# Attention heads and the closing stage of a two-layer trunk: one product moved ahead, value products in two banks, more banks and buffers at the end

## The chip, the cores and the metric

The kernel runs as one program on one core of a Trainium2 chip. The metric is the device time of one execution in microseconds (us), taken as the median of several runs. Five engines work side by side and are ordered by semaphores alone: TensorE (PE; its weight loads are shown apart as PEld), VectorE (DVE), ScalarE (ACT), GpSimd (POOL) and SyncE (SP), which here only issues DMA transfers.

## The reference

One step of a diffusion trunk with two layers over 128 prompt tokens and 512 sample tokens of width 1024, all in fp32. Layer 0 mixes by retention, layer 1 by attention; each is followed by a mixture of 16 experts, of which a router takes two for each token. Only the attention and the end of the step matter here.

```python
q = (rmsnorm(cq, q_norm) @ w_uq).reshape(B, T, MLA_HEADS, MLA_NOPE + MLA_ROPE)
...
k_nope = jnp.einsum('bkr,rhd->bkhd', ckv, w_uk)
v = jnp.einsum('bkr,rhd->bkhd', ckv, w_uv)
...
s = jnp.einsum('bqhd,bkhd->bhqk', qn, k_nope) + jnp.einsum('bqhd,bkd->bhqk', qp, kpe)
p = jax.nn.softmax(s.astype(F32) * scale, axis=-1).astype(v.dtype)
return jnp.einsum('bhqk,bkhd->bqhd', p, v)
...
return o @ w_o
...
xs = xs + g2s * grouped_moe(...)
y_sample = rmsnorm(xs, norm_final)
```

There are 8 heads of 128 columns (and 64 rotary ones), 640 tokens in five tiles of 128, the fifth being the prompt, which reads only its own 128 keys.

## The kernel before

The program is written engine by engine; each engine executes its list in order, and every `wait_ge` on a semaphore stands in that list. PSUM has eight banks of 512 fp32 columns, used under fixed numbers. The order of the work is written out by hand; there is no planner.

**A head of attention.** TensorE's list has for each head h three parts. `head_proj(h)` projects the queries of the 512 sample tokens into bank 1 (four steps of 128 rows, each two instructions of 512 columns, L1482); then the rotary queries into bank 2 (even heads alone, for two heads at once), the prompt's queries and the last 256 keys into bank 7, and the first 512 keys into bank 3. ScalarE (L1868, L1870) copies banks 1 and 3, VectorE banks 2 and 7 (for even heads with the rotation, L2476, then L2482 and L2487). `tail(h - 1)` closes the head before: the transposes of its fifth tile of probabilities and the value products of tiles 3 and 4. `main(h)` has the scores of the five tiles (L1513, L1514; even tiles in banks 0 and 1, odd ones in 2 and 3, the fifth only 128 columns in bank 0), the transposes of the first four tiles of probabilities (L1522, banks 4 and 5) and the value products of tiles 0 to 2 (L1532), in an order that puts other matmuls between a tile's scores and its transposes:

```python
score(h, 4)
prob_T(h, 3)
prob_v(h, 2)
```

is its end. Of a tile's softmax VectorE takes the maximum (L2493), ScalarE the exponential with its sum (L1878), TensorE transposes the result, ScalarE copies it out of PSUM (L1887), TensorE multiplies it by the values, and VectorE scales that by the reciprocal of the sum into `o_all` (`o_evac`, L2505). All value products are in bank 6, so each waits for the `o_evac` of the one before (`o_ev`). The SP list loads the next weights for keys and queries (`key_w`, `pair_w`) each time a head's projections are done.

**From the heads to the output projection.** After the tail of head 7, TensorE transposes `o_all` tile by tile into banks 2 and 3 (`o_T`, L1569); ScalarE and VectorE copy a half each (`oT_evac`, L1912 and L2539), and for each tile 32 instructions (L1581) project it into banks 4 and 5. VectorE's list has, between the last `o_evac` and its first `oT_evac`, `router_weights(1)` (L2011 to L2014). The SP list loads the gates' rows and the first expert's weights after the last value product (L672, L658 to L660).

**The last stage.** After the experts of layer 1, the SP list reads the sums back from DRAM into `x` (L707). The last expert's rows are spread by one-hot products, two banks for each tile in the pairs 4, 6, 2, 4, 6 (L1385); from the fourth tile on they wait for VectorE's add (`x_add`, L2393) to free a pair. ScalarE squares each tile (L1625), POOL makes the reciprocal root (`rstd`, L812 and L813), and VectorE's `final(t)` (L2409) scales the tile into one of two buffers, `fin`, which SP stores (L754). VectorE's list has all five adds first, then the five calls of `final`, each from the third on waiting until the store of its buffer's former tile has landed.

## Time and profile before

| what | value |
|---|---|
| runs of the kernel | 1773.40, 1774.48, 1776.93 us (median 1774.48) |
| span of the profiled execution | 1772.2 us |
| TensorE busy | 1684.3 us, 95% |
| VectorE, ScalarE, GpSimd busy | 705.7, 260.4, 184.0 us |
| attention heads | 1226 to 1444 us |
| output projection | 1449 to 1525 us |
| experts of layer 1 | 1555 to 1743 us |
| last stage | 1744 to 1772 us |

The profiled execution has its span alone on the page; how long that execution took as a whole is not shown. Times in the rows are counted from the start of the span. "Busy" is the time in which an engine had an instruction at work; matmuls overlap in a pipeline, so the time from one start to the next tells more than a matmul's own duration. An fp32 matmul shows as two instructions.

### The profile page before, as it was taken

To read this page: it belongs to the slowest core of one execution; us is meant where nothing else is said; L and a number is where in the kernel's file an instruction comes from. 1 tells how busy PE (TensorE), PEld (TensorE's weight loads), DVE (VectorE), ACT (ScalarE), POOL (GpSimd) and SP (SyncE) were. 2 spreads that over 40 slices of the span, in tenths; PEclk is the share of its full clock that TensorE was granted. 3 is DMA by queue.
4 is the path that set the end of the run, shared out by engine and by line. 5 is a ranking of instruction groups with operands and counts; after the bars stand their busy time and mean duration, and the time that the engine had idled before them with its cause. 6 is when DMAs were issued, how large, how long until landed. Compare 5 with 4: busy or idle time off the path is not lost.

```text
span 1772.2 us, 17375 instructions
## 1 busy us (share of the span) xinstructions
PE 1684.3 (95%) x6368; PEld 952.0 (54%) x6368; DVE 705.7 (40%) x1195; ACT 260.4 (15%) x554; POOL 184.0 (10%) x280
## 2 busy tenths in 40 slices
PE   5999999999999999999899999899999989999995
PEld 3864375644765465744464444354666654654442
DVE  1425533365333553255663232332233324533324
ACT  5100000000000000000121111322322321111111
POOL 2000100011000110001002222110000000022211
PEclk9999999999999999999999999999999999999998
DMA  8532561016410271103839999820000042579994
GB/s 320 204 142 95 199 224 48 0 48 235 156 47 0 95 286 57 47 0 141 256 149 307 351 339 329 273 100 3 22 25 11 0 120 95 201 244 343 340 329 143
DMA packets 159074, 280.21 MB, mean 158 GB/s; under 512 B 11396, under 2 KB 106392, under 8 KB 153896
## 3 DMA queue, kind: packets, MB, share of 16 engines
q1 hardware_dynamic: 144616, 236.39, 38.0%
q0 software_dynamic: 8960, 32.56, 7.0%
q10 hardware_dynamic: 5440, 10.49, 1.7%
q8 instruction: 36, 0.59, 0.1%
q14 instruction: 22, 0.18, 0.0%
HBM read 246.04 MB, written 33.37 MB: 158 GB/s over the span
## 4 chain that ended last, share of the span: by engine, by line
PE 79%; SPq 10%; DMA 4%; DVE 3%; issue 2%; ACT 2%; POOL 0%; DVEq 0%; POOLq 0%; ACTq 0%
PE banks L1085 11%; PE banks L1161 11%; PE banks L1060 8%; PE banks L1351 6%; SPq L659 5%; SPq L660 4%; PE banks L1482 4%; PE banks L1581 4%; PE banks L1157 3%; PE banks L1229 3%; PE banks L1368 2%; PE banks L1239 2%; PE banks L1217 2%; DMA wr<-in_moe_w_down 2%; PE banks L1513 2%; PE banks L1514 2%
## 5 line engine op out<-in xcount | busy, mean ns | idle before, releaser
L1351 PE MATMUL banks<-wr,arena 128*128 128x512 f32 x512 | 226.4, 595 | 10.8 <-DMA wr<-in_moe_w_down 10.1
L1161 PE MATMUL banks<-wr 128*128 128x512 f32 x432 | 191.4, 592 | 0.0
L1085 PE MATMUL banks<-wr 128*128 128x256 f32 x768 | 169.5, 379 | 0.0
L1351 PEld LDWEIGHTS banks<-wr,arena 128*128 128x128 f32 x512 | 94.6, 190 | 121.2 <-issue 118.9
L1085 PEld LDWEIGHTS banks<-wr 128*128 128x128 f32 x768 | 145.3, 190 | 22.7 <-issue 3.6
L1060 PE MATMUL banks<-wr,arena 128*128 128x512 f32 x320 | 143.4, 603 | 2.0 <-ACT arena L1688 2.0
L1161 PEld LDWEIGHTS banks<-wr 128*128 128x128 f32 x432 | 80.0, 190 | 91.2 <-issue 91.2
L1368 PE MATMUL banks<-wr,arena 128*128 128x512 f32 x256 | 115.4, 593 | 0.9 <-ACT arena L1804 0.9
L1060 PEld LDWEIGHTS banks<-wr,arena 128*128 128x128 f32 x320 | 60.5, 194 | 73.3 <-issue 72.3
L879 POOL DMA_INDIRECT acc_dram<-arena,put_ids x30 | 60.5, 2016 | 268.6 <-DVE arena L2363 268.6
L2348 DVE SCALAR_TENSOR_TENSOR arena<-banks,slot_w,arena 128x256 f32<-128x256 f32 x32 | 15.5, 484 | 173.6 <-ACT arena L1800 173.6
L2363 DVE TENSOR_TENSOR arena<-banks,arena 128x1024 f32<-128x1024 f32 x32 | 39.2, 1225 | 83.4 <-PE banks L1368 83.4
L1368 PEld LDWEIGHTS banks<-wr,arena 128*128 128x128 f32 x256 | 46.3, 190 | 48.3 <-issue 46.9
L1581 PE MATMUL banks<-wr,arena 128*128 128x512 f32 x160 | 70.2, 597 | 0.0
L829 POOL TENSOR_TENSOR arena<-arena 128x256 f32<-128x256 f32 x32 | 23.3, 733 | 377.6 <-DVE arena L2105 377.6
L2184 DVE BATCH_NORM_STATS2 st<-banks 128x6 f32<-128x512 f32 x40 | 28.0, 699 | 81.6 <-PE banks L1229 64.5
L2055 DVE TENSOR_TENSOR arena<-banks,arena 128x512 f32<-128x512 f32 x40 | 27.6, 691 | 82.3 <-PE banks L1060 82.2
L1229 PE MATMUL banks<-arena 128*128 128x512 f32 x128 | 60.1, 592 | 0.0
L1157 PE MATMUL banks<-wr 128*128 128x512 f32 x128 | 55.7, 593 | 0.0
L1482 PE MATMUL banks<-arena 128*128 128x512 f32 (+1 forms) x192 | 53.3, 434 | 1.1 <-DVE wr L2458 1.1
L1713 ACT ACTIVATE arena<-arena 128x512 f32<-128x512 f32 x24 | 15.1, 629 | 247.0 <-DVE arena L2164 114.1
L1581 PEld LDWEIGHTS banks<-wr,arena 128*128 128x128 f32 x160 | 30.4, 193 | 36.4 <-issue 36.4
(324 smaller groups left out, 2193.7 us busy)
## 6 DMA issues: line engine op xcount, KB each, us to landing
wr<-in_w_ada SPq DMA_DIRECT2D x24, 2048.0 KB, 7.6
wr<-in_moe_w_gate SPq DMA_DIRECT2D x32, 1024.0 KB, 14.2
wr<-in_moe_w_up SPq DMA_DIRECT2D x32, 1024.0 KB, 16.3
wr<-in_moe_w_down SPq DMA_DIRECT2D x32, 1024.0 KB, 15.6
wr<-in_ret_w_in SPq DMA_DIRECT2D x12, 2048.0 KB, 14.0
wr<-in_ret_w_in SPq DMA_DIRECT2D x8, 1024.0 KB, 11.7
wr<-in_ret_w_out SPq DMA_DIRECT2D x4, 2048.0 KB, 7.7
arena<-mod_rows_dram SPq DMA_DIRECT2D x14, 512.0 KB, 6.4
```

What stands on the lines that cost most here:

```text
L659: sp.dma_start(gu[:, :, 1, :], w_u[l][e]).then_inc(S(f"w_full{b}"), 16)
L660: sp.dma_start(dn, w_d[l][e]).then_inc(S(f"w_full{b}"), 16)
L879: g.indirect_dma_start(out=acc[l], out_offset=bass.IndirectOffsetOnAxis(ap=put_ids[:, e:e + 1], axis=0), in_=ysb[:, b, :], in_offset=None, ...
L1060: mm = mmul(bank[6 + hf][:], yT[:, t % 2, j, :], ring(slot)[:, j * D + hf * 512:j * D + hf * 512 + 512], start=(j == 0), stop=(j == 3))
L1085: mm = mmul(dst[:, r * 256:r * 256 + 256], lhs, rhs, start=(start and r == 0 and k == 0), stop=(k == 3), skip_group_check=True)
L1157: mm = mmul(dst, hT[:, k, TS:T], ring8(2 + int(tile))[:, k, :], start=(k == 0), stop=(k == KT - 1))
L1161: mm = mmul(dst, X[X_OF[p]][:, k, cols], W[p][:, k, :], start=(k == 0 and p not in ("P2", "P7", "P3")), stop=(k == 3), skip_group_check=True)
L1229: mm = mmul(bank[5][:], qd[:, u % 2, j, :], St[:, r, j, :], start=False, stop=(j == 1))
L1351: mm = mmul(bank[2][:], xgT[:, e.par, k, :], expert_w(e.buf)[0][:, k].rearrange("p g f -> p (g f)"), start=(k == 0), stop=(k == KT - 1))
L1368: mm = mmul(bank[4 + 2 * e.par + hf][:], gactT[:, e.par, j, :], expert_w(e.buf)[1][:, j, hf * 512:hf * 512 + 512], start=(j == 0), stop=(j ...
L1482: mm = mmul(dst, lhs(k), rhs(k), start=(k == 0), stop=(k == nk - 1))
L1581: mm = mmul(bank[4 + hf][:], oTb[:, t % 2, k, :], w_o[:, k, hf * 512:hf * 512 + 512], start=(k == 0), stop=(k == KT - 1))
```

## The change

It has four parts.

- `head_proj` is split: its stage 0, the query projection into bank 1 with the waits for the weights, moves into `main` of the head before, between the fifth score and the fourth transposes; stage 1 has the rest and, new, waits for the `o_evac` of tile 1.
- Value products use banks 6, 7, 6, 6, 7 (`PV_BANK`); each waits for the `o_evac` of the product that had its bank before, and that of tile 4 also for VectorE's evacuation of the next head's projections (`hp_d`), which share bank 7.
- After the last head, `o_T(0)` and the first `oT_evac` of ScalarE and VectorE come ahead of the tail, and `router_weights(1)` comes after VectorE's second `oT_evac`.
- In the last stage of layer 1 the bank pairs are 4, 6, 2, 0, 4, `fin` has five buffers, in tiles that are no longer used, and VectorE's list has `final(t - 2)` behind the add of tile t.

```diff
 V_BANK = (6, 7, 0, 1)
+PV_BANK = (6, 7, 6, 6, 7)
+LAST_BANK = ((4, 6, 2, 4, 6), (4, 6, 2, 0, 4))
...
+        def heads_d(h):
...
+            return 2 * h + 2
...
         def ring(s):
...
         fin_row = M["last"]
-        fin = M["xgT"].rearrange("p (b d) -> p b d", b=2)
+        fin = [xgT[:, 0].rearrange("p k n -> p (k n)"), xgT[:, 1].rearrange("p k n -> p (k n)"), xg[:, 0, :], xg[:, 1, :],
+               M["rows"][:, 0:D]]
...
                 dst = out[0][0] if t == PT else out[1][0, ORDER[t] * P:(ORDER[t] + 1) * P, :]
-                sp.dma_start(dst, fin[:, t % 2, :]).then_inc(S(f"fin_out{t % 2}"), 16)
+                sp.dma_start(dst, fin[t]).then_inc(S(f"fin_out{t % 2}"), 16)
             sp.wait_ge(S("fin_out0"), 48)
...
                 for t in range(NT):
-                    if t >= 3:
-                        pe.wait_ge(S("x_add"), 10 * RH + l * NT + t - 2)
-                    b0 = (4, 6, 2, 4, 6)[t]
+                    if t >= 3 + l:
+                        pe.wait_ge(S("x_add"), 10 * RH + l * NT + t - 2 - l)
+                    b0 = LAST_BANK[l][t]
                     for hf in range(2):
...
-            def head_proj(h):
+            def head_proj(h, stage_):
...
                 p, r = h % 2, h // 2
-                pe.wait_ge(S(f"wq_full{r % 2}"), r // 2 * 64 + 64)
-                pe.wait_ge(S(f"wk_full{p}"), r * 16 + 16)
+                if stage_ == 0:
+                    pe.wait_ge(S(f"wq_full{r % 2}"), r // 2 * 64 + 64)
+                    pe.wait_ge(S(f"wk_full{p}"), r * 16 + 16)
...
                 kn = lambda k: wk[:, p, k, :]
-                if h:
-                    pe.wait_ge(S("ex_done"), h * 5 - 2)
-                run(bank[1][:], qn, lambda k: cqT[:, k, 0:TS], 4).then_inc(S("hp_done"), 1)
+                if stage_ == 0:
+                    if h:
+                        pe.wait_ge(S("ex_done"), h * 5 - 2)
+                    run(bank[1][:], qn, lambda k: cqT[:, k, 0:TS], 4).then_inc(S("hp_done"), 1)
+                    return
                 if h:
                     pe.wait_ge(S("ex_done"), h * 5 - 1)
+                    pe.wait_ge(S("o_ev"), h * 5 - 3)
                     pe.wait_ge(S("hp_d"), h * 2)
...
                 pe.wait_ge(S("pt_a"), h.n * 5 + t + 1)
-                pe.wait_ge(S("o_ev"), h.n * 5 + t)
+                if h.n or t >= 2:
+                    pe.wait_ge(S("o_ev"), h.n * 5 + (-1, 0, 1, 3, 2)[t])
+                if t == 4 and h.n + 1 < MH:
+                    pe.wait_ge(S("hp_d"), heads_d(h.n + 1))
                 keys = [5] if t == PT else range(5)
...
                     rhs = V[:, kt, h.n * VD:h.n * VD + VD] if isinstance(h.n, int) else V[:, kt, bass.ds(h.n * VD, VD)]
-                    mm = mmul(bank[6][:, 0:VD], prT[:, gp, i, :], rhs, start=(i == 0), stop=(i == len(keys) - 1))
+                    mm = mmul(bank[PV_BANK[t]][:, 0:VD], prT[:, gp, i, :], rhs, start=(i == 0), stop=(i == len(keys) - 1))
                 mm.then_inc(S("pv_done"), 1)
...
                 score(h, 4)
+                if h.n + 1 < MH:
+                    head_proj(h.n + 1, 0)
                 prob_T(h, 3)
...
+            head_proj(0, 0)
             for h in range(MH):
-                head_proj(h)
+                head_proj(h, 1)
                 if h:
...
                 main(fixed(h, 2))
-            tail(fixed(MH - 1, 2))
-
-            pe.wait_ge(S("mw_o"), 16)
-            pe.wait_ge(S("o_ev"), 5 * MH)
...
             def o_T(t):
+                pe.wait_ge(S("o_ev"), 5 * MH - NT + t + 1)
+                if t == 0:
+                    pe.wait_ge(S("ex_done"), 5 * MH - 1)
                 if t:
...
             o_T(0)
+            tail(fixed(MH - 1, 2))
+            pe.wait_ge(S("mw_o"), 16)
             for t in range(NT):
...
                 main(fixed(h, 2))
-            probT_evac(fixed(MH - 1, 2), 4)
             act.wait_ge(S("cache_out"), 32)
...
             oT_evac(0)
+            probT_evac(fixed(MH - 1, 2), 4)
             oT_evac(1)
...
                     dve.wait_ge(S("op_done"), 10 * RH + l * NT + t + 1)
-                    v.tensor_tensor(x[:, t, :], x[:, t, :], banks((4, 6, 2, 4, 6)[t], 2), ALU.add).then_inc(S("x_add"), 1)
+                    v.tensor_tensor(x[:, t, :], x[:, t, :], banks(LAST_BANK[l][t], 2), ALU.add).then_inc(S("x_add"), 1)
+                    if l and t >= 2:
+                        final(t - 2)
...
                 else:
-                    for t in range(NT - 1):
-                        final(t)
+                    final(NT - 2)
+                    final(NT - 1)
...
                 dve.wait_ge(S("rstd"), 4 * NT + t + 1)
-                if t >= 2:
-                    dve.wait_ge(S(f"fin_out{t % 2}"), 16 * (t // 2))
-                v.scalar_tensor_tensor(out=fin[:, t % 2, :], in0=x[:, t, :], scalar=rs[:, t:t + 1], in1=fin_row,
+                v.scalar_tensor_tensor(out=fin[t], in0=x[:, t, :], scalar=rs[:, t:t + 1], in1=fin_row,
                                        op0=ALU.mult, op1=ALU.mult).then_inc(S("fin_ready"), 1)
...
                 dst = o_all[:, t, h.n * VD:h.n * VD + VD] if isinstance(h.n, int) else o_all[:, t, bass.ds(h.n * VD, VD)]
-                v.tensor_scalar(dst, bank[6][:, 0:VD], sm_inv[:, t:t + 1], None, ALU.mult).then_inc(S("o_ev"), 1)
+                v.tensor_scalar(dst, bank[PV_BANK[t]][:, 0:VD], sm_inv[:, t:t + 1], None, ALU.mult).then_inc(S("o_ev"), 1)
...
                 main(fixed(h, 2))
-            tail(fixed(MH - 1, 2))
-            dve.wait_ge(S("g1_in1"), 32)
-            router_weights(1)
...
             oT_evac(0)
+            tail(fixed(MH - 1, 2))
+            dve.wait_ge(S("g1_in1"), 32)
             for t in range(NT):
...
                     oT_evac(t + 1)
+                if t == 0:
+                    router_weights(1)
                 for hf in range(2):
...
             moe(1)
-            final(NT - 1)
```

## Rows read from the trace of the kernel before

**Rows 1.** The page: busy us (share of the span), number of instructions.

```profile
PE 1684.3 (95%) x6368; PEld 952.0 (54%) x6368; DVE 705.7 (40%) x1195; ACT 260.4 (15%) x554; POOL 184.0 (10%) x280
```

**Rows 2.** TensorE's waits in the heads: total us, times, longest us.

```profile
PE banks L1532 <- DVE wr L2505: 5.4, 9, 0.6
PE banks L1522 <- ACT arena L1887: 4.8, 8, 0.6
```

**Rows 3.** Timeline of TensorE at the turn to head 2: start, duration [idle before].

```profile
1276.37 0.39 PE L1514 MATMUL banks<-wr,arena 128*128 128x128 f32 x2
1277.35 0.74 PE L1522 MATMUL banks<-ident,arena 128*128 128x128 f32 x5 [0.60 <-ACT arena L1887]
...
1290.39 1.28 PE L1532 MATMUL banks<-wr,arena 128*128 128x128 f32 x10
1292.28 0.46 PE L1532 MATMUL banks<-wr,arena 128*128 128x128 f32 x2 [0.61 <-DVE wr L2505]
1292.58 1.02 PE L1513 MATMUL banks<-arena 128*128 128x512 f32 x2
1293.44 1.02 PE L1514 MATMUL banks<-wr,arena 128*128 128x512 f32 x2
```

**Rows 4.** Timeline of VectorE at the same turn.

```profile
1290.46 0.42 DVE L2487 COPY arena<-banks 128x256 f32<-128x256 f32 x1
```

**Rows 5.** Timeline of TensorE from the last head to the output projection.

```profile
1439.80 1.28 PE L1532 MATMUL banks<-wr,arena 128*128 128x128 f32 x10
1440.91 0.27 PE L1522 MATMUL banks<-ident,arena 128*128 128x128 f32 x1
...
1444.64 1.06 PE L1569 MATMUL banks<-ident,wr 128*128 128x128 f32 x8 [0.54 <-DVE wr L2505]
1447.36 1.94 PE L1569 MATMUL banks<-ident,wr 128*128 128x128 f32 x8 [1.65 <-DVE arena L2539]
1449.09 14.46 PE L1581 MATMUL banks<-wr,arena 128*128 128x512 f32 x32
1463.38 1.04 PE L1569 MATMUL banks<-ident,wr 128*128 128x128 f32 x8
```

**Rows 6.** Timeline of VectorE and ScalarE in the same stretch.

```profile
1441.18 0.35 DVE L2505 TENSOR_SCALAR wr<-banks,sm_inv 128x128 f32<-128x128 f32 x1 [1.98 <-PE banks L1532]
...
1445.80 0.60 ACT L1912 ACTIVATE arena<-banks 128x512 f32<-128x512 f32 x1 [4.30 <-PE banks L1569]
```

**Rows 7.** Windows: length, each engine's busy us, granted clock, DMA share, GB/s.

```profile
1226.00:1440.00 214.00, 203.91 (x1027) 137.75 (x1028) 71.86 (x204) 63.13 (x136) 0.00 (x0) 1.00 0.05 13
...
1448.00:1450.00 2.00, 2.00 (x9) 1.48 (x8) 0.67 (x1) 0.60 (x1) 0.00 (x0) 0.50 1.16 314
...
1555.00:1740.00 185.00, 180.62 (x532) 87.02 (x531) 58.35 (x79) 21.23 (x47) 43.13 (x29) 1.00 0.95 303
```

**Rows 8.** Timeline of the last stage, and its stores (KB, us to landing).

```profile
1751.81 3.77 DVE L2393 TENSOR_TENSOR x<-x,banks 128x1024 f32<-128x1024 f32 x3 [7.37 <-DMA x<-acc_dram]
1753.09 5.40 PE L1385 MATMUL banks<-arena 128*128 128x512 f32 x8 [3.17 <-DVE x L2393]
1756.12 1.22 DVE L2393 TENSOR_TENSOR x<-x,banks 128x1024 f32<-128x1024 f32 x1 [0.53 <-PE banks L1385]
1758.88 0.55 POOL L813 TENSOR_TENSOR rs<-rs,half 128x1 f32<-128x1 f32 x1
1763.85 2.49 DVE L2409 SCALAR_TENSOR_TENSOR arena<-x,rs,arena 128x1024 f32<-128x1024 f32 x2 [1.64 <-DMA out<-arena]
1767.88 1.28 DVE L2409 SCALAR_TENSOR_TENSOR arena<-x,rs,arena 128x1024 f32<-128x1024 f32 x1 [1.54 <-DMA out<-arena]
...
out<-arena SPq DMA_DIRECT2D x5, 512.0 KB, 2.7
```

**Rows 9.** Loads of query weights in the heads; TensorE's wait for expert weights.

```profile
arena<-in_mla_w_uq SPq DMA_DIRECT2D x4, 256.0 KB, 3.2
...
PE banks L1351 <- DMA wr<-in_moe_w_down: 3.2, 4, 1.3
```

## The prediction

> **What bounds the kernel now.** I read the page first: TensorE is busy for 1684.3 of 1772.2 us [rows 1], so what can be gained on this one core is either less work on TensorE or the stretches in which it stands still. The change takes no matmul away. It can only close gaps, so I looked for them with the view of TensorE's waits over the eight attention heads [rows 2]: two waits repeat with every head, both of about 0.60 us. One is L1522, the transposes of the fourth tile of probabilities, which wait for ScalarE's copy at L1887; the other is L1532, the last value product of a head, which waits for VectorE's evacuation at L2505. The timeline of TensorE then gives their size: the waits view counts from the modelled end of the matmul before, while the start-to-start distance also holds the refilling of the pipeline. Two 512-column instructions start 0.86 us apart from the next pair (1292.58 to 1293.44), so one takes 0.43; ten of 128 columns at 1439.80 are followed at 1440.91 by a transpose, so one takes 0.11 [rows 3, 5]. Where the starts are further apart than that, TensorE stood.
>
> The chain of waits leaves TensorE in two more places that the change touches: the passage from the last head to the output projection, 1439.80 to 1449.09 [rows 5], and the last 20 us after the experts [rows 8].
>
> **Next query projection ahead of the transposes (per turn between two heads).** Now: the last two score instructions start at 1276.37 and would be done issuing 0.22 later, at 1276.59; the transposes start at 1277.35, so 0.76 us is lost [rows 3]. After: the eight 512-column instructions of the next head's query projection, 8 x 0.43 = 3.44 us, stand in that gap. They need bank 1, which the third exponential has left free before the fifth score began (the score waits for the same count), and weights. ScalarE's copy that the transposes wait for needs only the 0.60 us [rows 2] beyond the score, so 3.44 us covers it; the projection is not extra, it leaves the block that follows. What it would cost uncovered is nothing new, the 0.76 would stay. The weight waits move earlier too, from after to before the transposes of the head before. The loads on the SP queue are still issued when the projection two heads back (keys) or two to three back (queries) is done, so a whole head's work, over 20 us, stands between issue and use; a 256 KB load lands in 3.2 us [rows 9]. I cost that at nothing. Gain 0.76 per turn.
>
> **Value products in two banks.** Now: ten products of tile 3 from 1290.39 could be followed at 1291.50; the two of tile 4 start at 1292.28, because both tiles use bank 6, and the score behind them at 1292.58 instead of 0.22 later: 0.78 + 0.08 = 0.86 us lost [rows 3]. After, tile 4 goes to bank 7, whose last value product was that of tile 1. But bank 7 also receives part of the next head's projection, so a new wait takes its place: for VectorE to have evacuated that (hp_d). At a turn to an even head that is the long one, with the rotary multiplications; its last copy is over at 1290.46 + 0.42 = 1290.88 [rows 4]. The product could start at 1291.50, 0.62 later, and the order of both engines from the rotary projection on is the same in the new kernel. So the wait costs 0; its bounds are 0 and the 0.86 that it replaces, and I take 0 by the 0.62. Behind it in TensorE's queue stand the next head's scores, which wait for the same evacuation anyway. At a turn to an odd head VectorE has two copies only, and ScalarE two copies, of which one of this width takes 0.60 [rows 6], twice that at most 1.20, against the 0.11 + 1.11 of the transpose and the tile 3 product: also nothing, but only just. The first product of the projection's second part also waits for tile 1's evacuation, whose product precedes the fifth score and now has another 3.44 us in front.
>
> Per turn 0.76 + 0.86 = 1.62 us; there are seven turns (the last head has no successor, its 0.76 stays): **11.3 us**. The lower bound is the waits alone, 2 x 0.60 x 7 = 8.5 [rows 2].
>
> **From the last head to the output projection.** Now, from the start of the tile 2 products at 1439.80, the first output matmul starts at 1449.09, 9.29 us [rows 5]. In it VectorE's router weights run ahead of its evacuation of the transposed output, which is why the second transposes start 1.65 us late. After, packed by the same rows: ten products 1.11, eight transposes 0.88, one transpose 0.11, ten products 1.11, two 0.22, eight transposes 0.88: 4.31 us. Can each start? The first transposes need heads' tile 0 and the fourth exponential: long done. Tile 3's products need VectorE's evacuation of tile 2, over at 1441.18 + 0.35 = 1441.53 [rows 6], and come at 1441.90. The first copies of the transposed output start 1.16 us after the transposes do (1444.64 to 1445.80) and take 0.60 [rows 5, 6]; ScalarE then copies the last probabilities before tile 4's product at 1443.01: 1440.91 + 1.16 + 0.60 + at most 0.60 is 1443.27, so 0 to 0.3 us may be lost. 9.29 - 4.31 = 4.98, less about 0.1: 4.9. VectorE's router weights, some 2 us, now stand behind the second evacuation; who waits for them is the router two tiles on, and VectorE's own first output evacuation 6.87 us later (16 x 0.43): nothing.
>
> Besides, the granted clock in 1448 to 1450 is 0.50, the 1.2 GHz level, after TensorE had stood for most of the 3 us before 1447 [rows 7, 5]. The first 32 output matmuls take 14.29 us from start to the next instruction instead of 32 x 0.43 = 13.76. With no such idle time before it I take the fall away: 0.5 us. Together **5.4 us**; lower bound 3.9, when the fall stays: the second transposes take 1.73 us start to start where eight take 0.88 [rows 5], so 0.85 + 0.5 of the gain goes, and a little more with the copies.
>
> The Trainium skill speaks against this step: TensorE: Matmul & The Clock Gate, Part 4 (PE-mode transpose), says that transposes do not count as activity for the clock, and the change packs sixteen more closely around the value products. By that rule the fall stays and the step gives the lower bound; here the transposes of the heads ran at a granted clock of 1.00 [rows 7], but between many matmuls. It is a rival below.
>
> SP's gate rows and the first expert's weights are released by the last value product, which now comes only 0.9 us before the output projection starts (in the packed order above, 0.88); their consumer, the normalised rows, comes only after the first output tile. I cost that at nothing.
>
> **The last stage.** Now VectorE adds three tiles from 1751.81, waits for TensorE, whose last eight matmuls need bank pairs that the adds free and run at half clock (5.40 us from 1753.09), and then writes five results in two buffers: the third waits until the first has left, 1763.85, the fifth starts at 1767.88 and ends at 1769.16 [rows 8]; a store lands in 2.7 us. After, four bank pairs let TensorE do four tiles at once; only the fifth waits, for the first add, and even at half clock its four matmuls are over by about 1755.8. Results follow their adds: from 1751.81 + 3.77 = 1755.58 VectorE has two adds of 1.22 to 1.26 and five results of 1.25 (2.49 for two), 8.7 us without a wait, to 1764.3. Its waits: tile 3's rstd came at 1758.88 + 0.55 = 1759.43, 2.1 us after that tile's add ended (1756.12 + 1.22) [rows 8]; in the new order tile 4's add ends about 1760.6, its rstd at 1762.7, before the result's turn at 1763.1; if ScalarE and POOL take a microsecond longer than that, the result starts at 1763.8 and ends at 1765.1. The five buffers lie in dead tiles, so no store is waited for. 1769.16 - 1764.3 = 4.8 at best; 3.5 when a handover of 0.1 us lies between each of the engine's steps and POOL is late; I take **4.5 us**, near the top, since VectorE's row of three adds shows no such gap.
>
> **Does the gain reach the end?** Between lie the experts, where TensorE is busy 180.62 of 185 us and DMA 0.95 [rows 7]; TensorE waited 3.2 us for weights there [rows 9]. Each expert's load but the first few is issued on the end of an earlier expert's products, and those few on marks of the output projection, so the stream starts earlier by what TensorE does: I carry the gain whole.
>
> **Sum.** 11.3 + 5.4 + 4.5 = 21.2 us. The profiled span 1772.2 becomes 1751.0. The median of the three runs is 1774.48, 2.3 us above the span; the page gives only the span of its execution, and I leave that difference as it is: 1774.48 - 21.2 = **1753.3 us**.
>
> **Rivals.** (a) The new wait for VectorE takes the place of the old one at every turn: 7 x 0.86 = 6.0 us stays, 1759.3. For: the odd turns are nearly even in the sum above; against: 0.62 of slack at even turns. Chance 0.08. (b) The clock falls at the passage all the same: 5.4 becomes 3.9, 1754.8; 0.07. (c) The experts' DMA stream, not TensorE, sets the end, and swallows what is gained ahead of it: only the last stage's 4.5 remains, 1770.0. For: DMA 0.95 there; against: every load is released by TensorE. 0.04. (d) Slower: the denser attention loses TensorE's full clock. Each us of work at the lower of the two levels costs another us, half rate; from 21 us of the heads' 204 on, a tenth, the gain is gone; a quarter would cost 51 us and give 1804. Against: 180.62 busy of 185 ran at 1.00 [rows 7]. 0.02. (e) The query projection does not cover its gap, because the wait is for something behind it: 7 x 0.76 = 5.3 stays, 1758.6; 0.03.
>
> **How the numbers follow.** The forecast has 0.76. Its terms' bounds: gain 8.5 + 3.9 + 3.5 = 15.9 to 11.3 + 5.5 + 4.8 = 21.6, so 1758.6 to 1752.9; the three runs lie up to 2.4 us off their median, which I add on both sides: 1750.5 to 1761.0. That takes in (a), (b) and (e) as well. This kernel's measurement can tell about 0.2%, 3.5 us, from no change. Faster by more: the forecast, (a), (b), (e) and half of (c), 0.96; I keep 0.95. Within: 0.03. Slower: (d), 0.02.
>
> **What would show it.** In the profile after, L1522 and L1532's successors should be gone from TensorE's waits but for the last head; a turn from an odd to an even head, and back, should take about 1.6 us less; the first output matmul should start some 4.3 us after the last head's tile 2 products, at a clock of 1.00; VectorE's last result should show no wait for a store. It is wrong if TensorE's new waits name VectorE's copies of the projection, if the experts take longer by what was gained, or if the clock row shows a fall in attention.

## The result, and the profile after

The changed kernel takes 1753.62 us (median; 1752.46 to 1754.49), the kernel before 1774.76 us beside it (1773.4 to 1776.93): a ratio of 0.9886, with a 95% interval of 0.987 to 0.9902. Forecast were 1753.3 us.

Both kernels have the same marks in their timelines, so the span can be cut at them. Each difference of the table is start to start, from the first instruction named to the next mark (us):

| stretch | before | after | difference | forecast |
|---|---|---|---|---|
| start to head 0's projection | 1226.36 | 1227.44 | +1.08 | 0 |
| heads, to the last head's tile 2 products | 213.4 | 202.0 | -11.4 | -11.3 |
| passage, to the first output matmul | 9.29 | 4.32 | -4.97 | -4.9 |
| output projection and router, to the experts | 106.0 | 105.4 | -0.6 | -0.5 |
| experts, to the last products | 189.4 | 189.5 | +0.1 | 0 |
| last products to VectorE's first add | 7.31 | 7.15 | -0.2 | 0 |
| first add to the last result's end | 17.35 | 12.89 | -4.46 | -4.5 |
| last result's end to the span's end | 3.04 | 4.17 | +1.13 | 0 |
| span | 1772.2 | 1752.9 | -19.3 | -21.2 |

The profiled execution of the changed kernel is the one that took 1754.49 us, its slowest; that is a part of why its span falls by less than the median.

TensorE's row of the page answers [rows 1]: its busy time is 5.7 us less, while the span is 19.3 us less. No matmul went, so what went is mostly standing time.

```profile
PE 1678.6 (96%) x6368; PEld 950.4 (54%) x6368; DVE 704.6 (40%) x1195; ACT 259.7 (15%) x554; POOL 184.8 (11%) x280
```

TensorE's waits in the heads of the changed kernel (total us, times, longest), to be read beside [rows 2]: of the seventeen listed there, one is left, that of the last head, which has no successor to project. The other two are at head 0, where no head precedes, and were there before too.

```profile
PE banks L1490 <- DVE wr L2476: 1.1, 1, 1.1
PE banks L1524 <- ACT arena L1888: 0.7, 1, 0.7
PE banks L1533 <- ACT arena L1905: 0.6, 1, 0.6
```

The turn to head 2 in the changed kernel, TensorE, then VectorE and ScalarE, answers [rows 3] and [rows 4]. The projection's eight instructions (L1490) start 0.22 us after the last scores, the transposes (L1533) right behind them. Tiles 3 and 4 are one unbroken group of twelve products, which begins at 1289.05; its last two start ten times 0.11 us later, at 1290.16. VectorE's copy, for which they now wait, was over at 1289.53, 0.63 us ahead, where the forecast had 0.62. ScalarE's copy of the last probabilities, for which they waited in the kernel before too, was over later, at 1289.90: 0.26 us ahead.

```profile
1275.82 0.39 PE L1525 MATMUL banks<-wr,arena 128*128 128x128 f32 x2
1276.04 3.60 PE L1490 MATMUL banks<-arena 128*128 128x512 f32 x8
1279.47 0.71 PE L1533 MATMUL banks<-ident,arena 128*128 128x128 f32 x5
...
1289.05 1.50 PE L1546 MATMUL banks<-wr,arena 128*128 128x128 f32 x12
1290.39 1.02 PE L1524 MATMUL banks<-arena 128*128 128x512 f32 x2
```

```profile
1289.11 0.42 DVE L2505 COPY arena<-banks 128x256 f32<-128x256 f32 x1
...
1289.63 0.27 ACT L1905 ACTIVATE arena<-banks 128x128 f32<-128x128 f32 x1
```

The passage, TensorE (answers [rows 5]): no wait stands between the tile 2 products at 1429.45 and the first output matmul. The two groups of output transposes (L1585) take 0.87 and 0.88 us to the next start, the 32 output matmuls 13.73 instead of 14.29.

```profile
1429.45 1.28 PE L1546 MATMUL banks<-wr,arena 128*128 128x128 f32 x10
1430.57 1.04 PE L1585 MATMUL banks<-ident,wr 128*128 128x128 f32 x8
1431.44 0.27 PE L1533 MATMUL banks<-ident,arena 128*128 128x128 f32 x1
1431.55 1.50 PE L1546 MATMUL banks<-wr,arena 128*128 128x128 f32 x12
1432.89 1.04 PE L1585 MATMUL banks<-ident,wr 128*128 128x128 f32 x8
1433.77 13.90 PE L1599 MATMUL banks<-wr,arena 128*128 128x512 f32 x32
1447.50 1.04 PE L1585 MATMUL banks<-ident,wr 128*128 128x128 f32 x8
```

Windows of the heads, the passage and the experts (columns as in [rows 7]): the granted clock, third number from the end, is 1.00, the 2.4 GHz level, through the heads and the passage; the experts are as full as before.

```profile
1227.00:1429.00 202.00, 200.28 (x1021) 136.04 (x1022) 71.27 (x205) 62.09 (x134) 0.00 (x0) 1.00 0.05 13
1429.00:1447.00 18.00, 18.00 (x75) 10.66 (x75) 5.67 (x15) 2.36 (x6) 0.00 (x0) 1.00 0.79 206
...
1539.00:1724.00 185.00, 180.52 (x533) 87.13 (x532) 58.26 (x79) 21.23 (x47) 43.24 (x29) 1.00 0.95 303
```

The last stage (answers [rows 8]): TensorE, VectorE, and GpSimd's two steps for the last tile. No result waits for a store any more. The last one waits 0.71 us for GpSimd, whose first step took 1.17 us for this tile instead of the 0.19 it takes for most; in the kernel before it took 1.17 for the last tile, too.

```profile
1737.11 1.98 PE L1392 MATMUL banks<-arena 128*128 128x512 f32 x4 [1.29 <-DVE x L2411]
...
1744.27 2.47 DVE L2427 SCALAR_TENSOR_TENSOR arena<-x,rs,arena 128x1024 f32<-128x1024 f32 x2
1747.45 1.28 DVE L2427 SCALAR_TENSOR_TENSOR arena<-x,rs,arena 128x1024 f32<-128x1024 f32 x1 [0.71 <-POOL rs L820]
...
1745.61 1.17 POOL L819 TENSOR_SCALAR rs<-ss 128x1 f32<-128x1 f32 x1 [1.51 <-ACT arena L1643]
1746.87 0.55 POOL L820 TENSOR_TENSOR rs<-rs,half 128x1 f32<-128x1 f32 x1
```

### The profile page after: what moved, and what is told of

It is laid out like the page before. It is cut to its first block, busy times and chain, and to the rows that moved or that the text cites. A ratio compares the mean times of both kernels' runs of the same rounds, so it can differ in the third digit from the quotient of the medians.

```text
span 1752.9 us, 17372 instructions
## 1 busy us (share of the span) xinstructions
PE 1678.6 (96%) x6368; PEld 950.4 (54%) x6368; DVE 704.6 (40%) x1195; ACT 259.7 (15%) x554; POOL 184.8 (11%) x280
## 4 chain that ended last, share of the span: by engine, by line
PE 81%; SPq 10%; DMA 4%; DVE 2%; issue 1%; ACT 0%; POOL 0%; POOLq 0%; DVEq 0%; ACTq 0%
PE banks L1092 11%; PE banks L1168 11%; PE banks L1067 8%; PE banks L1358 6%; SPq L666 5%; PE banks L1490 4%; PE banks L1599 4%; SPq L667 4%; PE banks L1164 3%; PE banks L1236 3%; PE banks L1375 3%; PE banks L1246 2%; PE banks L1224 2%; PE banks L1524 2%; PE banks L1546 2%; PE banks L1525 2%
## 5 line engine op out<-in xcount | busy, mean ns | idle before, releaser
L1358 PEld LDWEIGHTS banks<-wr,arena 128*128 128x128 f32 x512 | 94.7, 190 | 120.1 <-issue 117.6
L1067 PEld LDWEIGHTS banks<-wr,arena 128*128 128x128 f32 x320 | 59.8, 191 | 71.2 <-issue 70.8
L1375 PEld LDWEIGHTS banks<-wr,arena 128*128 128x128 f32 x256 | 46.3, 190 | 48.3 <-issue 46.9
L1490 PE MATMUL banks<-arena 128*128 128x512 f32 (+1 forms) x192 | 54.5, 434 | 1.1 <-DVE wr L2476 1.1
L2511 DVE TENSOR_REDUCE smx<-banks 128x1 f32<-128x640 f32 (+1 forms) x40 | 28.7, 718 | 52.2 <-PE banks L1525 52.0
```

What stands on the lines that cost most here:

```text
L1067: mm = mmul(bank[6 + hf][:], yT[:, t % 2, j, :], ring(slot)[:, j * D + hf * 512:j * D + hf * 512 + 512], start=(j == 0), stop=(j == 3))
L1358: mm = mmul(bank[2][:], xgT[:, e.par, k, :], expert_w(e.buf)[0][:, k].rearrange("p g f -> p (g f)"), start=(k == 0), stop=(k == KT - 1))
L1375: mm = mmul(bank[4 + 2 * e.par + hf][:], gactT[:, e.par, j, :], expert_w(e.buf)[1][:, j, hf * 512:hf * 512 + 512], start=(j == 0), stop=(j ...
L1490: mm = mmul(dst, lhs(k), rhs(k), start=(k == 0), stop=(k == nk - 1))
```

## The experiments

The runs of one kernel spread by some microseconds (the first below by 1765.8 to 1773.5), and in the profiles head 0's projection starts between 1224.9 and 1231.2 us, though the code ahead of it is the same in all. So a part worth 3 us is read from the marks of its stage, and the totals only bear the sum. In e2_banks they do so loosely: its total fell by 9.9 us, its one profile, of its slowest execution (1770.82), gives 5.7 without the start, and where the others gained more is not shown. All in us; an interval is that of the ratio to the kernel before, timed beside it:

| kernel | total | ratio, interval | heads | passage | output projection to experts | first add to last result | to the end |
|---|---|---|---|---|---|---|---|
| before | 1774.76 | 1 | 213.4 | 9.29 | 106.0 | 17.35 | 3.04 |
| after | 1753.62 | 0.9886, 0.987 to 0.9902 | 202.0 | 4.32 | 105.4 | 12.89 | 4.17 |
| e1_q0 | 1769.46 | 0.9968, 0.9951 to 0.9985 | 208.0 | 9.28 | 106.0 | old | old |
| e2_banks | 1764.01 | 0.9945, 0.9929 to 0.9961 | 207.5 | 8.55 | 106.3 | old | old |
| e3_turn | 1760.08 | 0.9916, 0.9889 to 0.9943 | 202.0 | 7.72 | 103.8 | old | old |
| e4_passage | 1768.26 | 0.9983, 0.9971 to 0.9995 | 213.5 | 5.16 | 103.8 | old | old |
| e5_last | 1771.41 | 0.9992, 0.9981 to 1.0004 | 213.5 | 9.29 | 106.0 | 12.83 | 4.15 |
| e6_slack | 1758.09 | one run | 208.2 | 4.31 | 103.8 | new | new |
| e7_router_first | 1756.21 | one run | 202.1 | 5.51 | 105.4 | new | new |
| e8_router_later | 1774.98 | one run | 213.5 | 8.58 | 106.3 | old | old |
| e9_oT_earlier | 1750.31 | 0.987, 0.9845 to 0.9894 | 202.3 | 4.17 | 102.4 | 12.84 | 4.19 |
| e10_rstd | 1752.38 | 0.9886, 0.987 to 0.9902 | 202.0 | 4.31 | 103.8 | 12.38 | 3.38 |
| e11_fill | 1751.22 | 0.9884, 0.9867 to 0.99 | 202.0 | 4.31 | 102.4 | 12.82 | 4.15 |
| e12_all | 1751.93 | 0.9881, 0.9866 to 0.9897 | 202.3 | 4.18 | 103.6 | 12.29 | 3.37 |

"Old" and "new" are within 0.3 us of before and after; in e9_oT_earlier and e12_all the heads take in the first output transposes, which the passage then lacks. The theory throughout is the prediction's: each gap closes by its own part, and the gains add and reach the end.

**The two parts of the turn, alone and together.** e1_q0 is the kernel before with the projection split and its first half moved:

```diff
                 score(h, 4)
+                if h.n + 1 < MH:
+                    head_proj(h.n + 1, 0)
                 prob_T(h, 3)
```

> The kernel before with one part alone: the next head's query projection ahead of the fourth transposes; value products stay in one bank, the passage and the last stage as before. My theory (each of the two gaps of a turn is closed by its own edit): the stretch from the first projection of head 0 to the last head's tile 2 products, 213.4 us before and 202.0 in the changed kernel, shrinks by 7 x 0.76 = 5.3 to 208.1; the wait of the transposes stays once, for the last head, and the wait of the tile 4 products stays 8 times. Total time 5.3 us less, ratio 0.997. Rival (the gap only moves to the next wait): the stretch stays within 1 us of 213.4.

e2_banks is the kernel before with the value products in two banks and the wait that this brings:

```diff
-                    mm = mmul(bank[6][:, 0:VD], ...
+                if t == 4 and h.n + 1 < MH:
+                    pe.wait_ge(S("hp_d"), heads_d(h.n + 1))
+                    mm = mmul(bank[PV_BANK[t]][:, 0:VD], ...
```

> The kernel before with one part alone: value products in banks 6 and 7, with the waits that this needs; the query projection where it was. My theory: the tile 4 product no longer waits, 7 x 0.86 = 6.0 us less in the heads (213.4 to 207.4); in the passage, too, the tile 4 product of the last head follows at once, another 0.8. Ratio 0.996. Rival (VectorE's evacuation of the next head's projection takes the place of the wait): TensorE's waits name it, and the heads stay at 213.4 or shrink by only the 4 odd turns' share, 3.4.

e3_turn has both edits.

> Both edits of the turn, without those of the passage and of the last stage. My theory: the two gains add: heads 213.4 to 202.0 as in the changed kernel, 11.4 us, and 0.8 in the passage; ratio 0.993. Rival (they share a gain, or need each other): less than the sum of the two runs with one edit each, or more.

Measured in the heads: -5.4, -5.9 and -11.4. The gains add, as the gaps lie at different places of a turn. TensorE's waits show that each part removes just its own wait: in e1_q0 the products' is left (first row), in e2_banks the transposes' (second row).

```profile
PE banks L1541 <- DVE wr L2518: 5.4, 9, 0.6
```

```profile
PE banks L1532 <- ACT arena L1902: 4.8, 8, 0.6
```

**The passage and the last stage, alone.** e4_passage is the kernel before with the first output transposes ahead of the last head's tail and the other engines' order to match; e5_last has only the bank pairs, the five buffers and the results behind their adds.

```diff
+            o_T(0)
             tail(fixed(MH - 1, 2))
             pe.wait_ge(S("mw_o"), 16)
...
-            o_T(0)
```

> The kernel before with the passage alone: first transposes of the output ahead of the last head's tail, router weights behind the second evacuation; heads and last stage as before, value products in one bank. My theory: from the last head's tile 2 products to the first output product 9.29 us become 4.31 + 0.78 (the tile 4 product still waits for the tile 3 evacuation) = 5.1, and the clock does not fall, 0.5 more: 4.7 us less in all, ratio 0.9973. Rival (transposes let the clock fall): the granted clock reads 0.50 around the second transposes and the gain is about 3.2.

```diff
-                    b0 = (4, 6, 2, 4, 6)[t]
+                    b0 = LAST_BANK[l][t]
...
+                    if l and t >= 2:
+                        final(t - 2)
```

> The kernel before with the last stage alone: four bank pairs, five buffers, results between the adds. Of the span, from the first add's start to the end, 20.4 us before, 17.1 in the changed kernel. My forecast was 4.5 us less, the changed kernel's one profile shows 3.3. If the 1.1 us between the last store's landing and the end of the span that the changed kernel shows belong to the new order, they are here again: 3.3 us less. If they were that one execution's, 4.4 us less. Ratio 0.9975 to 0.998.

The passage took 5.16; the 0.84 above the full change is the wait for bank 6, which this kernel keeps. In e5_last the stage from the first add shrinks by 4.52, but the end comes 1.1 later behind it, so 3.4 net; of that the total shows 0.4, with 3.4 at the edge of its interval. The 1.1 us therefore belongs to the new last stage, not to the rest of the change.

**How much slack the new wait leaves.** e6_slack is the changed kernel with idle copies ahead of the evacuations that the last value product waits for: 1, 3 and 8 on VectorE at the turns to heads 2, 4 and 6, 1 and 2 on ScalarE at those to heads 3 and 5.

```diff
+                for _ in range({2: 1, 4: 3, 6: 8}.get(h, 0)):
+                    ch.link(v.tensor_copy(mtmp[:, 0:128], bank[7][:, 0:128]))
                 v.tensor_copy(knT[:, p, 512:768], bank[7][:, 256:512])
```

> The changed kernel with idle copies put ahead of the last copy of a head's projection: on VectorE 1 for head 2, 3 for head 4, 8 for head 6 (128 columns from bank 7, 0.29 us and about 0.07 for the handover, so 0.35, 1.1 and 2.9 us); on ScalarE 1 for head 3 and 2 for head 5 (512 columns, 0.67 and 1.3 us). Theory: the tile 4 product behind the turn has 0.63 us in hand at even turns and about 0.2 at odd ones, so it waits 0, 0.5 and 2.3 us at heads 2, 4 and 6, and 0.5 and 1.1 at heads 3 and 5; in total 4.4 us more than the changed kernel. Rival (the evacuation is not what the tile 4 product would wait for next): no wait at heads 2 to 4, and where there is one it sits at the next head's scores.

The heads took 6.2 more. TensorE at four turns (at the first and the last with the tile 3 products ahead), then VectorE at the last of them:

```profile
1310.19 1.28 PE L1546 MATMUL banks<-wr,arena 128*128 128x128 f32 x10
1311.73 0.49 PE L1546 MATMUL banks<-wr,arena 128*128 128x128 f32 x2 [0.26 <-ACT arena L1907]
...
1339.83 0.46 PE L1546 MATMUL banks<-wr,arena 128*128 128x128 f32 x2 [0.33 <-DVE arena L2509]
...
1364.13 0.49 PE L1546 MATMUL banks<-wr,arena 128*128 128x128 f32 x2 [0.88 <-ACT arena L1907]
...
1390.63 1.28 PE L1546 MATMUL banks<-wr,arena 128*128 128x128 f32 x10
1393.86 0.46 PE L1546 MATMUL banks<-wr,arena 128*128 128x128 f32 x2 [1.95 <-DVE arena L2509]
```

```profile
1390.69 2.57 DVE L2508 COPY arena<-banks 128x128 f32<-128x128 f32 x8
1393.29 0.42 DVE L2509 COPY arena<-banks 128x256 f32<-128x256 f32 x1
```

Eight copies put off VectorE's last copy by 2.60 us (from 1390.69 to 1393.29). The two products behind it, due 1.11 after the ten, at 1391.74, start at 1393.86, 2.12 late: so 0.48 us of the 2.60 was slack. Three copies (0.98) make the products 0.50 late, 0.48 again; one copy (0.32) leaves no wait. The forecast's 0.62 is more, as it has the products start the moment that the copy ends, and here they start 0.15 behind it (1393.71 to 1393.86). On ScalarE a copy (0.63) makes them 0.43 late and two (1.25) 1.05: slack 0.20. The listed waits are 0.17 shorter than these delays, as they count from the modelled end of the ten products.

So the new wait, for VectorE, is real, and it starts to cost at 0.48 us at even turns. That for ScalarE at the odd turns is another, for the last probabilities, which the kernel before had too; with 0.20 it is the nearer one, and by the row of 1289.63 above it is no further off at the turn to head 2. The four waits make 3.4 us, and each costs another 0.25 or so for the refilling, 4.4 together, as expected. The rest is the clock, which the expectation didn't have: from the scores behind the last of these waits to the next transposes it took 6.09 us, 4.35 in the changed kernel, 1.7 more. Behind the stand of 1.95 us the granted clock was 0.62 and 0.52 (windows of the same kernel).

```profile
1394.00:1396.00 2.00, 2.00 (x5) 1.08 (x6) 0.65 (x2) 0.00 (x0) 0.00 (x0) 0.62 0.03 8
1396.00:1398.00 2.00, 2.00 (x6) 0.99 (x5) 0.00 (x0) 0.00 (x0) 0.00 (x0) 0.52 0.00 0
```

**Where the passage's gain lies, and its clock.** e7_router_first is the changed kernel with VectorE's router weights again ahead of its first evacuation; e8_router_later is the kernel before with them behind its second.

```diff
+            dve.wait_ge(S("g1_in1"), 32)
+            router_weights(1)
...
-                if t == 0:
-                    router_weights(1)
```

> The changed kernel with VectorE's router weights ahead of its first evacuation of the transposed output again. VectorE is then done with that evacuation about 1.4 us later, and TensorE stands for 1.4 us in one piece before the second transposes. Theory (the clock fell in the kernel before because TensorE stood, 3.3 us in four pieces of 6.4): with 1.4 us of standing it stays at 1.00, and the first output product comes 1.4 us later than in the changed kernel, 5.7 us behind the tile 2 products. Rival (any standing here makes it fall): the clock reads 0.50 and another 1 to 1.5 us go.

```diff
-            router_weights(1)
...
+                if t == 0:
+                    router_weights(1)
```

> The kernel before with only the router weights moved behind VectorE's second evacuation. The second transposes then start 0.7 us earlier (ScalarE's and VectorE's copies take 0.60 and 0.68 side by side); TensorE stands 2.6 us there instead of 3.3. Theory: standing decides the clock, and 2.6 us in four pieces is still most of it, so it still falls: 0.7 us less in all. Rival (VectorE's order was the whole cause): clock 1.00 and about 2 us less.

The order of the router weights is worth 1.2 us in the changed kernel (5.51 against 4.32, for 1.4 expected; the second transposes wait 1.00) and 0.7 in the kernel before (8.58 against 9.29; their wait falls from 1.65 to 0.94). In e8_router_later the clock still falls, to 0.50 in 1449 to 1451; in e7_router_first it doesn't. Nor do the stands of the passage alone decide. In e2_banks and e3_turn TensorE stands for 0.50, 0.64 and 1.65 us at the same distances, and yet the second transposes run at half clock in the one (first row) and at the full clock in the other (second row):

```profile
1443.43 1.94 PE L1584 MATMUL banks<-ident,wr 128*128 128x128 f32 x8 [1.65 <-DVE arena L2555]
```

```profile
1436.00 1.06 PE L1586 MATMUL banks<-ident,wr 128*128 128x128 f32 x8 [1.65 <-DVE arena L2557]
```

What differs is the heads ahead, where e2_banks still stands at each turn. What sets the fall is left open; that the packed passage has none is shown by after, e4_passage, e7_router_first and e9_oT_earlier.

**A gap that the change left.** e9_oT_earlier is the changed kernel with the first output transposes ahead of the last head's fourth ones, to fill the 0.60 us there.

```diff
                     head_proj(h.n + 1, 0)
+                else:
+                    o_T(0)
                 prob_T(h, 3)
```

> The changed kernel with the first transposes of the output one place earlier still, ahead of the last head's fourth transposes, where TensorE still stands for 0.76 us (the last head has no successor whose projection could stand there). Theory: eight transposes, 0.88 us, cover it; TensorE's wait there disappears, and from the last head's fifth score to the first output product 0.7 us less, which no comparison of times can tell, but the trace can. Ratio to the kernel before 0.988. Rival: the transposes wait for the fourth exponential, which ends just as the fifth score does, or the evacuation behind them delays the last probabilities: the wait only moves.

The gap closed, and its gain was given back two steps later: tile 3's products, with no transposes between, now come before VectorE has emptied bank 6.

```profile
1430.09 1.57 PE L1546 MATMUL banks<-wr,arena 128*128 128x128 f32 x12 [0.50 <-DVE wr L2525]
```

From the first projection to the first output matmul it took 206.5, the changed kernel 206.3. That this profile was shorter is due mostly to the stretch behind, 102.4 instead of 105.4, whose code is the same, and to an earlier start (1225.9). There the router's matmuls end and TensorE waits for VectorE's selection (L1311); in the changed kernel the clock falls behind that wait, where nothing covers it; in e9_oT_earlier it falls ahead of it (0.63 and 0.51 in 1514 to 1518), where TensorE would have waited for VectorE anyway.

**Filling that wait.** e11_fill is the changed kernel with 14 idle products instead of 6 ahead of it.

```diff
-                idle_products(IDLE_BANK[l], 6)
+                idle_products(IDLE_BANK[l], 14 if l else 6)
```

> The changed kernel, with 14 idle products instead of 6 ahead of TensorE's wait for the second layer's selection (each about 0.22 us by the rows, together 1.8 of the 2.0 us wait). Theory (the fall of the clock behind that wait costs what the stretch from the output projection to the experts varies by): TensorE no longer stands there, the granted clock does not fall behind it, the 16 idle instructions after it take 2.0 instead of 3.7 us and the gathers' first 40 take 4.7 instead of 5.6; the stretch falls from 105.4 to 102.4 to 102.9 and the total by about 2.6 us. Rival (the clock falls whatever is done with the wait, for a reason in the router's short products before it, and comes late back): the stretch stays at 105 to 106 and the total with it.

The stretch took 102.4, as expected. TensorE in the changed kernel, then in e11_fill, with a window of each:

```profile
1522.59 0.45 PE L1311 MATMUL banks<-arena,before 128*128 128x80 f32 x2 [2.00 <-DVE arena L2306]
...
1524.62 3.70 PE L928 MATMUL banks<-ident 128*128 128x128 f32 x16
...
1524.00:1528.00 4.00, 4.00 (x20) 4.00 (x20) 2.82 (x13) 0.00 (x0) 0.00 (x0) 0.50 1.00 315
```

```profile
1521.97 0.45 PE L1311 MATMUL banks<-arena,before 128*128 128x80 f32 x2 [0.22 <-DVE arena L2306]
...
1523.38 1.99 PE L928 MATMUL banks<-ident 128*128 128x128 f32 x16
...
1523.50:1527.50 4.00, 4.00 (x37) 3.90 (x36) 3.51 (x16) 0.00 (x0) 0.00 (x0) 1.00 0.99 326
```

In total 3 us in one stretch can't be told from the changed kernel: the intervals of the two ratios overlap nearly whole.

**The end.** e10_rstd is the changed kernel with the last tile's reciprocal root taken off GpSimd.

```diff
+            A_(rs[:, NT - 1:NT], ss[:, NT - 1:NT], ACT.Sqrt, scale=1.0 / D, bias=epsc[:]).then_inc(S("oTa"), 1)
...
+                    dve.wait_ge(S("oTa"), NT + 1)
+                    ch.link(v.reciprocal(rs[:, t:t + 1], rs[:, t:t + 1]))
```

> The changed kernel, with the last tile's reciprocal root taken off GpSimd: ScalarE takes the square root right after its sum of squares, VectorE the reciprocal. GpSimd's last work is then tile 3's. In the changed kernel the span ends 4.17 us after the last result, in the kernel before 3.04. Theory (GpSimd's closing instruction): the rows show a DRAIN of 5.83 us on GpSimd's queue at the program's end, begun at 1746.88 in the changed kernel, so done at 1752.71 and only then the span ends at 1752.88, while the last store has landed by 1751.6; in the kernel before it was done at 1768.18, before the last store. With tile 3 as GpSimd's last it begins at about 1743.6 and is hidden again: the tail falls from 4.17 to 3.0 to 3.1, and the last result begins 0.4 to 0.5 earlier (VectorE's own results end at 1746.73, plus a reciprocal of 0.16). Total gain over the changed kernel about 1.6 us. Rival (the new order of the stores, or five buffers, cost the 1.1): the tail stays at 4.1 to 4.2, and the gain is 0.5 us.

The closing instruction of GpSimd's queue (duration in ns, start), in before, after and e10_rstd:

```profile
L187 POOLq DRAIN  x1: 5834/5834/5834, 1762.3 to 1762.3; - x1
```

```profile
L189 POOLq DRAIN  x1: 5832/5832/5832, 1746.8 to 1746.8; - x1
```

```profile
L189 POOLq DRAIN  x1: 5832/5832/5832, 1741.5 to 1741.5; - x1
```

It ends at 1768.2, 1752.7 and 1747.4; the spans end at 1772.2, 1752.9 and 1749.5. Only in the changed kernel is it the last thing. With it out of the way the tail fell from 4.17 to 3.38 (3.0 to 3.1 expected), and the last result came 0.5 earlier, as expected. Of the 1.1 us, 0.8 is shown to be this; the tail stayed 0.3 above the kernel before's, between the last two steps of the closing barrier, and why is open. The total again can't tell 1.3 us.

**All together.** e12_all is e9_oT_earlier with the edits of the last two.

> The kernel with the first output tile's transposes ahead of the last head's fourth ones (it took 1750.3 us, its stretch from output projection to experts 102.4) with both edits of the two kernels before: the last reciprocal root off GpSimd and 14 idle products. By the theories of those two: 1.6 us less at the end; nothing more from the idle products, since this kernel's clock fell earlier, beside VectorE's selection, where it cost nothing. So about 1748.7 us, a ratio to the kernel before of about 0.9855, and heads plus passage unchanged at 206.4 to 206.5. Rival: if the place of the fall is a matter of chance in each run, the stretch may be anywhere from 102.4 to 106 and the total from 1748.7 to 1752.

The total, 1751.93, missed the expected 1748.7. The profile has the expected end (12.29 and 3.37), but the stretch to the experts took 103.6, not 102.4. In e9_oT_earlier the fall of the clock had already slowed TensorE so far that it waited only 0.31 us for the selection, so the sixteen idle instructions more, 1.76 us, ran past it: from the router's first sum (L1303) to L1311 it took 8.34 us instead of 7.02. No kernel here is faster than the changed one by more than the intervals.

## Why the prediction was right

- **The turn between heads: right.** Forecast 1.62 per turn and 11.3 in all, measured 11.4. Both gaps closed whole, each by its own part (e1_q0 5.4 for 7 x 0.76 = 5.3, e2_banks 5.9 for 7 x 0.86 = 6.0). Rival (e) falls with e1_q0.
- **The new wait at nothing: right, and now with a size.** Of the 0.62 at even turns 0.48 can be used (e6_slack). Of the odd turns the prediction said only just, and there 0.20 is left; but that is ScalarE's old wait, not the new one, and the prediction did not price it at even turns, where it is as near. Rival (a), which names VectorE, was 0.48 us away at three of the seven turns; at the last odd one VectorE's copies are over 2.1 us ahead of the products (1412.61 for 1414.73).
- **The passage: right.** 4.32 for 4.31 plus 0.1; the possible 0 to 0.3 us for ScalarE's copies did not show. The clock was worth 0.56 in the output matmuls, for 0.5; that this belongs to the passage is not shown, for these matmuls took 13.90 also in e3_turn, with the heads changed and the passage as before. Rival (b) fell: with sixteen transposes around the value products the granted clock stayed at 1.00 in the changed kernel, and the first 32 output matmuls took the same 13.90 (by their row) in every kernel with the packed passage. The rule of the Trainium skill (TensorE: Matmul & The Clock Gate, Part 4: PE-mode transpose) is not thereby refuted, since the value products make up half of the stretch, but what I drew from it for this kernel did not happen. The reason that the prediction gave for the fall, the standing time just ahead, is not enough either (e2_banks against e3_turn).
- **The last stage: the term right, a step missing behind it.** From the first add to the last result's end 4.46 went, for 4.5. The result waited 0.71 us for GpSimd, within the bounds set for that. That 4.5 was hit all the same is in part luck: the sum's 4.8 less 0.71 is 4.1, and VectorE's steps behind the first three adds, 1.13 to 1.21 us from start to start for the 1.22 to 1.26 of the sum, gave 0.3 back. But the prediction ended its sum at the last result and took the tail of 3.04 as fixed. The timelines leave closing instructions out (the view of the line that they carry shows them), and GpSimd's, 5.83 us long, had 4.0 us of cover in the kernel before; shortening the last stage by 4.5, with GpSimd's last step 0.5 later behind the first add than before (11.03 against 10.53), used that up. So the stage gave 3.3, not 4.5.
- **The gain reaches the end: right.** Experts 189.4 and 189.5. Rival (c) falls with it, and so does (d): the heads ran at 1.00.
- **The sum.** The marks give -20.4 without the start (-11.4, -4.97, -0.6, +0.1, -0.2, -4.46, +1.13), for -21.2. That the median lies 0.3 us from the forecast is in part chance, as the spread of the start and of the router's clock is larger than that.

## What to carry to other kernels

A wait that repeats in every turn of a loop is filled with work that the next turn needs anyway, and what its price is can be read from start-to-start distances rather than from the listed idle time; then look up by how much the wait that takes its place is early, and every other wait of the same instruction, for the least slack is what the next edit may use (0.20 here, not 0.62). When a last stage is shortened, list each engine's closing instructions too: the engine that finished early may have been covered only by what is now gone. Filling one gap in front of a chain of other engines moves the wait behind it unless that chain is shorter (e9_oT_earlier, e12_all).

## What the runs showed of the hardware

- GpSimd's closing DRAIN took 5.83 us in every kernel listed. It begins with the engine's last instruction and outlasts it: in the changed kernel that one (1746.87, 0.55 us) ended at 1747.42, the DRAIN at 1752.7, 5.3 us later. VectorE's and ScalarE's (1.32 and 1.18 us, from 1747.5 and 1744.4) also begin with the engine's last work, but end within 0.1 us of it (1748.73 and 1745.53); SyncE's took 0.013. The Trainium skill (VectorE: DVE Perf Modes, The DRAIN you can't avoid) gives the DRAINs from before and after a kernel as about 12 ns on all engines. SyncE's agrees, GpSimd's does not, and the measurement decides.
- Behind a stand of 1.95 us in the heads the clock read 0.62 and 0.52, the 1.2 GHz level for most of that time, which cost 1.7 us besides the wait; behind one of 0.88 it stayed at 1.00 (e6_slack). One of 2.00 in the router phase cost 1.4 to 3.0 us (103.8 in e10_rstd and 105.4 in after, against 102.4 where it was filled); where the fall came ahead of the wait, it cost nothing.
- With equal code the stretch from the output projection to the experts took 105.4 us in one profile (after) and 103.8 in another (e10_rstd, changed only at the end), by when the full clock came back (at about 1530.1 and 1526.9). What sets that is open.
